# A two-layer encoder on one core: two Fourier sums and the token rows move to GpSimd, and the router, the first weight split and the final norm are reordered

## The reference, cut to what matters

```python
# layer 0
hn = rms_norm(h, norm_mix[0])
u = (hn @ w_in).reshape(B, S, 4, 256)
h = h + fft2(u, axes=(1, 3), norm="ortho").real.reshape(B, S, D) @ w_out
hn = rms_norm(h, norm_ffn[0]);  h = h + (silu(hn @ w_gate) * (hn @ w_up)) @ w_down
# layer 1
hn = rms_norm(h, norm_mix[1]);  h = h + neighbourhood_attention(hn, w_qkv, rpb, w_o)
hn = rms_norm(h, norm_ffn[1])
logits = hn @ w_router + b_router                 # 8 experts
top_val, top_idx = top_k(logits, 2);  gates = softmax(top_val)
h = h + sum over the two experts of gate * (silu(hn @ w_gate[e]) * (hn @ w_up[e])) @ w_down[e]
return rms_norm(h, final_norm)
```

## Time and profile before

| | us |
|---|---|
| median of 3 runs (1365.29 to 1366.33) | 1365.94 |
| the profiled execution, its own time | 1367.15 |
| its span from first to last instruction | 1365.3 |
| TensorE busy in the span | 1344.7 |
| VectorE, ScalarE, GpSimd busy | 1111.9, 923.2, 34.5 |

### The profile page before, as it was taken

The page is one execution under the profiler, slowest core; times in us unless marked ns, Lnnn a source line. Parts: engine busy times, 40 slices in busy tenths (PEclk is TensorE's granted clock), DMA queues, the critical chain, the costliest instruction groups (busy, mean ns, idle before and its releaser), DMA issues.

```text
span 1365.3 us, 17406 instructions
## 1 busy us (share of the span) xinstructions
PE 1344.7 (98%) x6341; PEld 1117.9 (82%) x6341; DVE 1111.9 (81%) x815; ACT 923.2 (68%) x755; POOL 34.5 (3%) x48
## 2 busy tenths in 40 slices
PE   8999999999999999999999999999999999999997
PEld 7888888787878888888888888888888888888885
DVE  5756666655678889888988988898898889889997
ACT  6554444545647778777777877877787787777774
POOL 0000000000101000000000000000000000002000
PEclk8999999999989999999999999999999999999999
DMA  9666775563339999999999999999999999999992
GB/s 354 246 207 179 210 211 190 175 204 104 101 109 378 383 378 365 395 382 357 398 388 372 373 394 377 358 398 388 368 376 394 367 370 397 381 374 385 396 394 90
DMA packets 194971, 432.32 MB, mean 317 GB/s; under 512 B 19632, under 2 KB 22064, under 8 KB 194800
## 3 DMA queue, kind: packets, MB, share of 16 engines
q1 hardware_dynamic: 178784, 416.28, 83.4%
q0 software_dynamic: 3360, 11.78, 2.2%
q10 hardware_dynamic: 12784, 3.69, 1.8%
HBM read 425.94 MB, written 5.78 MB: 316 GB/s over the span
## 4 chain that ended last, share of the span: by engine, by line
PE 95%; DVE 3%; ACT 1%; issue 1%; DMA 0%; POOL 0%; DVEq 0%; ACTq 0%
PE bank_G L1250 10%; PE bank_G L1252 10%; PE bank_G L1251 10%; PE bank_U L1250 10%; PE bank_U L1252 10%; PE bank_U L1251 10%; PE bank_Y L1250 8%; PE bank_Y L1252 8%; PE bank_Y L1251 8%; PE bank_T L1696 2%; PE bank_T L1250 1%; PE bank_T L1252 1%; PE bank_T L1251 1%; DVE w_lo L753 1%; PE bank_G L1512 0%
## 5 line engine op out<-in xcount | busy, mean ns | idle before, releaser
L753 DVE TENSOR_TENSOR w_lo<-raw,w_hi 128x2048 fp32r<-128x2048 f32 x390 | 885.9, 2289 | 184.6 <-ACT w_hi L458 183.8
L458 ACT ACTIVATE w_hi<-raw 128x2048 fp32r<-128x2048 f32 x390 | 748.6, 1920 | 276.6 <-PE bank_U L1252 98.2
L1250 PE MATMUL bank_Y<-w_hi,hidT_hi 128*128 128x512 f32 x492 | 192.2, 391 | 0.0
L1252 PE MATMUL bank_Y<-w_hi,hidT_lo 128*128 128x512 f32 x492 | 191.6, 389 | 0.0
L1251 PE MATMUL bank_Y<-w_lo,hidT_hi 128*128 128x512 f32 x492 | 191.5, 389 | 0.0
L1250 PE MATMUL bank_U<-w_hi,xg_hi 128*128 128x512 f32 x448 | 179.1, 400 | 0.0
L1250 PE MATMUL bank_G<-w_hi,xg_hi 128*128 128x512 f32 x448 | 175.2, 391 | 1.3 <-DVE xg_lo L774 0.9
L1252 PE MATMUL bank_U<-w_hi,xg_lo 128*128 128x512 f32 x448 | 175.0, 391 | 0.0
L1251 PE MATMUL bank_U<-w_lo,xg_hi 128*128 128x512 f32 x448 | 174.5, 390 | 0.0
L1252 PE MATMUL bank_G<-w_hi,xg_lo 128*128 128x512 f32 x448 | 174.5, 390 | 0.0
L1251 PE MATMUL bank_G<-w_lo,xg_hi 128*128 128x512 f32 x448 | 174.4, 389 | 0.0
(11 more groups left out here) (301 smaller groups left out, 1363.5 us busy)
## 6 DMA issues: line engine op xcount, KB each, us to landing
raw<-in_expert_w_gate SPq DMA_DIRECT2D x112, 1024.0 KB, 7.7
raw<-in_expert_w_up SPq DMA_DIRECT2D x112, 1024.0 KB, 7.8
raw<-in_expert_w_down SPq DMA_DIRECT2D x112, 1024.0 KB, 7.7
raw<-in_nat_w_qkv SPq DMA_DIRECT2D x12, 1024.0 KB, 5.1
raw<-in_ffn_w_gate SPq DMA_DIRECT2D x11, 1024.0 KB, 8.9
raw<-in_ffn_w_up SPq DMA_DIRECT2D x11, 1024.0 KB, 5.7
raw<-in_ffn_w_down SPq DMA_DIRECT2D x11, 1024.0 KB, 5.2
raw<-in_fourier_w_out SPq DMA_DIRECT2D x4, 1024.0 KB, 15.6
```

The costliest lines, as they stand in the source:

```text
L458: nc.scalar.activation(w_hi[w][:], raw[s][:], ACT.Copy).then_inc(hi_made, 1)
L753: nc.vector.tensor_tensor(w_lo[w][:], raw[s][:], w_hi[w][:].bitcast(f32), ALU.subtract).then_inc(lo_made, 1)
L1250: nc.tensor.matmul(out_, xh, wh, start=start, stop=False)
L1252: return nc.tensor.matmul(out_, xl, wh, start=False, stop=stop)
```

## The change

Seven edits. (1) 23 matmuls on zeros in place of 12. (2) VectorE's split of piece 5 moves from before the second `u_lo` to behind the rests of `token_dft` 0 to 3. (3) `token_dft` writes four banks in turn and `channel_dft` one of its own for each group; the sums over tokens are done by GpSimd. (4) The first product of a stream waits for each quarter by itself. (5) The router: the gain goes into the router's weights, the stream goes token block by token block between the `w_o` products (one of its four groups of transposes stands in the middle of `last_wo_product`), the logits of a block start when it is there, the splits of two later pieces come after the choice of slots, and more `keep_warm` matmuls run. (6) The normed rows `hn` are made by GpSimd, two instructions for each token block, before the first expert's gather. (7) In expert 7 the last weight piece is split by column halves and the first half of the result is scattered before the second is complete; the gain is multiplied in early by VectorE and the final scale is applied by ScalarE; three of six small weight instructions come later.

```diff
@@ start and Fourier part @@
-        still(12)
+        still(23)
@@ vector
-            split_past(at["w_in"][c][-1])
+            split_past(at["w_in"][c][-1] - c)
...
-            even, odd = Y[g % 2][:, :S], fo["odd"][:, g % 2]
+            even, odd = BY_CHANNEL[g][:, :S], fo["odd"][:, g % 2]
...
-            for n, op in enumerate((ALU.add, ALU.subtract)):
-                nc.vector.tensor_tensor(tokens[:, :, n], channels[:, :, 0], channels[:, :, 1], op).then_inc(ft_tokens, 1)
...
+            if g == 1:
+                split_past(at["w_in"][1][-1])
             if g >= 2:
+                dve.wait_ge(ft_tokens, 2 * (g - 1))
@@ gpsimd
+        rstds(0)
+        for g in range(GROUPS):
+            channels, tokens = fo["by_channel"][:, g % 2], fo["by_token"][:, g % 2]
+            pool.wait_ge(ft_channels, 2 * (g + 1))
...
+            for n, op in enumerate((ALU.add, ALU.subtract)):
+                nc.gpsimd.tensor_tensor(tokens[:, :, n], channels[:, :, 0], channels[:, :, 1], op).then_inc(ft_tokens, 1)
@@ tensor
-            if m >= 2:
-                pe.wait_ge(pt_lo_done, m - 1)
+            if m >= 4:
+                pe.wait_ge(pt_lo_done, m - 3)
@@ tensor, project()
+                        if stream is not None and b == 0 and kk % 2 == 0:
+                            pe.wait_ge(act_lo_done, 4 * stream + kk // 2 + 1)
@@ rows, gpsimd (before: line 1205 on vector)
+        for b in range(NB):
+            pool.wait_ge(rstd_done, 3 + b + 1)
+            pool.wait_ge(h_half, 4 + 2 * b + 2)
+            nc.gpsimd.tensor_scalar(hn[:, b], h[:, b], rstd[:, 3, b:b + 1], None, ALU.mult).then_inc(hn_scaled, 1)
+            pool.wait_ge(hn_scaled, b + 1)
+            nc.gpsimd.tensor_tensor(hn[:, b], hn[:, b], mo["gain"][:, 0], ALU.mult).then_inc(hn_made, 1)
@@ router, tensor
+        wo_product(0, 1, 0)
+        wo_product(1, 1, 0)
+        transpose_tokens_of(0, 0)
+        wo_product(0, 1, 1)
+        transpose_tokens_of(0, 1)
+        last_wo_product()
         pe.wait_ge(rw_lo_done, 1)
+        logits(0, 0)
+        transpose_tokens_of(1, 1)
+        logits(0, 1)
+        logits(1, 0)
+        logits(1, 1)
+        keep_warm(12)
...
-        keep_warm(2)
+        keep_warm(5)
@@ router, vector
+        nc.vector.tensor_tensor(mo["rw"][:], mo["rw"][:], gains[:, 3].unsqueeze(2).to_broadcast([P, KD, NE]), ALU.mult).then_inc(rw_scaled, 1)
...
+        add_wo(0, 0)
+        split_past(W0 + 2)
+        add_wo(0, 1)
+        squares_of_rest(0)
+        tokens_lo(0, 0)
+        token_lo(0, 0)
+        add_wo(1, 0)
+        tokens_lo(0, 1)
+        token_lo(0, 1)
+        tokens_lo(1, 0)
+        add_wo(1, 1)
+        squares_of_rest(1)
+        tokens_lo(1, 1)
@@ expert 7, tensor
+            if kept:
+                last_columns(0, 4)
+                last_columns(1, 2)
+                scatter(0)
+                last_columns(1, 2, 2)
...
+            if kept:
+                scatter(1)
@@ end, scalar
+        for q in range(2):
+            for b in range(NB):
+                act.wait_ge(e_added, NB * q + b + 1)
...
+                nc.scalar.activation(mo["hn_hi"][:, b, cs], h[:, b, cs], ACT.Square, accum_out=total).then_inc(fin_sq, 1)
+        for b in range(NB):
+            act.wait_ge(fin_rstd, b + 1)
+            for q in range(2):
...
+                nc.scalar.activation(part, part, ACT.Copy, scale=rstd[:, 4, b:b + 1]).then_inc(fin_scaled, 1)
@@ end, vector
-                nc.vector.scalar_tensor_tensor(out=hn[:, b, cs], in0=h[:, b, cs], scalar=rstd[:, 4, b:b + 1],
-                                               in1=mo["gain"][:, 1, cs], op0=ALU.mult, op1=ALU.mult).then_inc(fin_done, 1)
+            nc.vector.tensor_tensor(FINAL[b][:, cs], h[:, b, cs], mo["gain"][:, 1, cs], ALU.mult).then_inc(fin_gain, 1)
```

More of the change, by code:

```diff
@@ L1160, in expert @@
                     hidden_rest(E, c - 1)
+                if (kind, c, half) == ("gate", STEPS - 1, 1) and kept and not sweep:
+                    gate_weights()
                 if (kind, c, half) == ("gate", 1, 1) and ahead and not sweep:
@@ L1252, in three, with project @@
             return nc.tensor.matmul(out_, xl, wh, start=False, stop=stop)
-        def project(pieces, banks, width, done, before=lambda n, b: None):
+        def project(pieces, banks, width, done, before=lambda n, b: None, stream=None):
             for n, j in enumerate(pieces):
@@ L1720, in down, with last_columns, scatter @@
                 last.then_inc(piece_used, 1)
+            def last_columns(q, rows, first=0):
+                c = STEPS - 1
+                if first == 0:
+                    ready(AT["down", c, 0], E)
+                    pe.wait_ge(e_hidT_lo, E * STEPS + (c + 1))
+                for kk in range(first, first + rows):
+                    half, k = kk // KROW, kk % KROW
+                    j = AT["down", c, half]
+                    if q == 0 and half and k == 0:
+                        pe.wait_ge(lo_half, E - LAST + 1)
+                    if q == 1 and half and k == 0:
+                        ready(j, E)
+                    wh, wl = parts(j, E, KROW)
+                    cs = slice(BANK * q, BANK * (q + 1))
+                    last = three(Y[q][:], hidT_hi[c % 2][:, P * kk:P * (kk + 1)], hidT_lo[c % 2][:, P * kk:P * (kk + 1)],
+                                 wh[:, k, cs], wl[:, k, cs], False, kk == BANK // P - 1)
+                    if q and k == KROW - 1:
+                        last.then_inc(piece_used, 1)
+                    elif kk == BANK // P - 1:
+                        last.then_inc(e_y, 1)
+            def scatter(q):
+                pe.wait_ge(e_selT_copy, E - LAST + 1)
+                pe.wait_ge(e_ylo, 2 * (E - LAST) + 1 + q)
+                for b in range(NB):
+                    cs = slice(BANK * q, BANK * (q + 1))
+                    bk = T[q] if b == 0 else (G, U)[q][1]
+                    nc.tensor.matmul(bk[:], mo["selT"][:, b], mo["y_hi"][:, cs], start=True, stop=False)
+                    nc.tensor.matmul(bk[:], mo["selT"][:, b], mo["y_lo"][:, cs], start=False, stop=True).then_inc(e_scatter, 1)
             for c in range(STEPS):
```

303 lines of the change are left out of this document (167 added, 136 removed).

## The result

| | us |
|---|---|
| before, median of 8 runs | 1365.76 |
| after, median of 8 runs (1368.80 to 1372.45) | 1370.65 |
| ratio, 95% interval | 1.0032, 1.0023 to 1.0041 |
| profiled execution of after: own time, span | 1369.09, 1367.3 |

The change makes the kernel slower by 3.1 to 5.6 us. The forecast was 1360.0 with a range to 1366.8: wrong in sign, and outside the range.

What follows compares the result with a forecast made beforehand. TensorE, busy 1344.7 of 1365.3 us, was taken as the bound. Gains 2.25 - 1.2 + 0.85 + 3.7 + 0.4 + 0 = 6.0 were to bring the median from 1365.94 to 1360.0; own range 1357.5 to 1363, stated range 1357.8 to 1366.8.

Steps and rivals of the forecast that it cites:

- The normed rows: Router: GpSimd makes them in 6 us (bounds 3.8 to 7.5) beside VectorE's chain, which keeps its pace; cost 0.
- Rival 1: Router: GpSimd holds up VectorE's chain, nine instructions with two SBUF inputs; router loses 2.5, total 1366.2; chance 0.32.
- Rival 3: Router: GpSimd's rows take 9, VectorE is held until 398, router loses 5 or more; total 1369; chance 0.10.
- The router: Logits end earlier, `used` comes 3.0 earlier and the gather runs at full clock: gain 3.7.
- The start: More zero matmuls keep the clock at 2.4 GHz, so the Fourier part begins at 31.0, not 33.28: gain 2.25.
- The Fourier part: After the start: TensorE waits 1.05 for the last two groups and starts `w_out` 0.13 later: loss 1.2.
- GpSimd's 0.6 an instruction: Fourier part: assumed price of each GpSimd sum over tokens, between 0.38 (gain 0.3) and 0.94 (loss 3.9).
- the ring: Fourier part: each group passes `fold`, GpSimd's two sums, `act_hi`, `act_lo` and handovers, 3.35 us a round.
- The moved split: Fourier part: 2.3 us of VectorE work before the first `fold`, giving back part of what the start gives.
- Waits by quarters: At 257, first product of a stream: two `act_lo` suffice instead of four, removing most of a 1.36 wait: gain 0.85.
- Expert 7: Three of six weight instructions move away from TensorE's 0.4 wait for `w_lo`: gain 0.4, between 0 and 0.42.
- the end: After the last product: 0.95 lost to early scatter, 0.4 and 0.44 gained, 0 to 0.6 for GpSimd's root: taken as 0.

Runs made afterwards that it cites:

- E1: The changed kernel with the normed rows back on VectorE: median 1365.79, 0.9999 of before.
- E8: The kernel before with only the normed rows moved to GpSimd and VectorE's two instructions removed: median 1371.23, 1.0031 of before.
- E5: The changed kernel with both the normed rows and the Fourier sums by token back on VectorE: median 1363.45, 0.9977 of before.
- E2: The changed kernel with the Fourier sums by token back on VectorE: median 1369.24, 1.0020 of before.
- E3: The changed kernel with the final scalings back on VectorE behind the root, without early gain products: median 1370.32, 1.0027 of before.
- E4: The changed kernel run again unchanged, for a second profile: median 1371.17, 1.0030 of before.
- E6: As E5, with the weight split of piece 5 back in front of the second `u_lo`: median 1363.42, 0.9978 of before.
- E9: As E5, with the first half's scatter back behind the last down products: median 1364.25, 0.9986 of before.
- E10: As E5, with 12 zero matmuls at the start in place of 23: median 1365.67, 0.9996 of before.
- E15: The kernel before with 23 zero matmuls at the start in place of 12, nothing else: median 1366.02, 0.9997 of before.
- E16: E5's kernel run again unchanged: median 1363.58, 0.9976 of before.
- E13: As E5, with scatter behind the last down products, last scalings on VectorE and both `y_lo` ahead of the adds: median 1362.21, 0.9972 of before.
- E7: The changed kernel with GpSimd's normed rows held back until VectorE's last `hn_lo`: median 1367.58, 1.0008 of before.

## Why the prediction was wrong, point by point

- **The normed rows, "at 0", is the step that failed.** I wrote that "VectorE's chain runs at its own pace, at 0". It costs 4.2 to 5.4 us in the time (E1), 4.2 put into the kernel before by itself (E8). Two things were wrong in it. The direction: from one row in which GpSimd gave way to VectorE I took it that VectorE never does. It was the case in which VectorE had started first. The price: the four instructions take 10.4 us in place of 6, over my upper bound of 7.5 and my rival's 9, so that GpSimd is busy until 398.4, and its second product also meets `slot`, behind `used`; `sel` meets the clearing of `no_row` that follows.
- **The rivals.** Rival 1 had the mechanism, but counted only the nine instructions with two SBUF inputs; `slot` (and `sel`), `tensor_scalar` with one input, were held too. With 1366.2 it was short by 4.4. Rival 3 (0.10) had the price and the direction, 1369 against 1370.65, though not the sum: it had the router lose 5 and the rest gain 2.3. The Trainium skill's "SBUF — State Buffer", "Who interferes with whom", weighed in the forecast, was right where I set the row above it: of two engines on the shared pair the one that starts second waits, and `tensor_scalar` may take that pair as well. The trace agrees for GpSimd's product (`eq` and `slot` end with it) and for `tensor_reduce`, which was never held; GpSimd's scaling of 2.84 us, however, held VectorE only to its first 1.1.
- **The router, 3.7: right without the rows.** E1 gains 3.9 against the profile of before, E5 5.1. The chain took 3.0 for my 3.4. But the clock did not stay up: it fell within the logits or behind them in most profiles of the new router, for 3 to 7 us (some 10 in E2, and twice in E3 and E4), at another moment each time (E5, E6 and E9 kept it). And in the profiles with the rows on VectorE 1.4 to 1.7 are given back before the last result row, which I had not in the sum.
- **The start, 2.25: right for that execution, not for each.** 30.91 for 31.0 forecast. Against the profiles E8 and E10 it is 1.3, and by itself, with two banks, it gives no gain clear of noise (E15). With the rest of the change in place it is worth more than its stage shows, 2.6 by the ratios of E10 and E5; in E10's profile 1.3 of it stands at the start and the rest in a longer router, where the clock was low for 6.8 us (3.2 in E16); whether its other executions are like that, and why, these runs don't tell.
- **The Fourier part, loss 1.2: 2.8.** One mis-sized term is GpSimd's 0.6 an instruction: 0.72, eight of them, and the ring went round in 3.63 for 3.35, which makes about 1.0 of the 1.6. The rest is not GpSimd's price: with the sums on VectorE the loss is 0.6 (E2), where I had a gain of 0.3 for 0.38 an instruction. There TensorE waits 0.29 and 1.56 for `pt_lo` and starts the product with `w_out` 14.1 behind the first Fourier product, where the kernel before took 13.5. The moved split, which I blamed for "what the start gives", is worth nothing that can be measured either way (E6).
- **Waits by quarters, 0.85: 0.67.** Both first `act_lo` were enough, as forecast: the wait fell from 1.36 to 0.58.
- **Expert 7, 0.4, and the end, 0: together a loss of 1.2.** The 0.4 wait is gone, and up to the last product E13 is 0.7 shorter than the kernel before. For the end my own terms add up to a loss of 0.1 to 0.7, of which I took 0. By the profiles the early scatter put the last product off by 1.35 (E13 against the changed kernel) where I gave 0.95. From the end of the scatter to the last scaling it gained 0.3 where I had credited 0.84. And the last transfers landed 3.4 us behind the last scaling in place of 2.6, a term that I didn't have; E5 and E16, with the same end, have 2.7, so it isn't the end's edit alone. E13 shows that the order of before was the better one.
- **The sum.** Second profile of after against the profile of before: 2.3 - 2.8 + 0.7 - 2.8 - 0.1 - 1.2 = -3.9 by the rounded stages. The medians differ by 4.9, since the profiled execution of before stood 1.4 above its median and this one of after 0.4 above 1370.65. Between the 6.0 of the forecast and this -3.9 lie 9.9 us: 6.5 in the router, which is what taking the rows off GpSimd gives back there (6.6 in E1), 1.6 in the Fourier part and 1.6 in expert 7 and the end.

## What to carry to other kernels

Before work goes to GpSimd, write down which VectorE instructions run in the same microseconds, and count its single-input `tensor_scalar` among those that can be held; work that is free by its own dependences can sit on the critical path through what the two engines share. Here 2.5 us of VectorE work (the two `hn` instructions in E5), behind the last urgent split, was 4 to 5 us cheaper than 10.4 us on an "idle" engine. A short row that grows to the end of another engine's row shows it; the list of waits has only TensorE's longer wait for `sel`, not its cause. And take a gain from one profile's low clock with care: 3.4 and 6.8 us at half clock came from the same instructions.

The best kernel of the study is E13 (23 zero matmuls, four banks, waits by quarters, the new router, rows and sums on VectorE, the old end): 1362.21, 0.9972 of before, with an interval to 0.9984, and 0.6% under the changed kernel. E5, with only rows and sums back, has 0.9977.

## What the runs showed of the hardware

- GpSimd's `tensor_scalar` of 128 x 1024 with one scalar for each partition took 2.85, longer than its `tensor_tensor` of two such inputs, 2.36; 128 x 256 with two inputs took 0.72.
- VectorE's small instructions with two SBUF inputs, and its `tensor_scalar` with one, were held to the end of GpSimd's `tensor_tensor` (up to 2.27 of its 2.36; `tensor_reduce` was not), but only for the first 1.1 of its `tensor_scalar` (in the changed kernel, E4 and E8: VectorE's instruction starts within 0.1 of it and takes 1.06), and in the changed kernel VectorE then ran nine small instructions at full pace beside the rest of it. The other way, GpSimd's `tensor_scalar` was stretched from 2.86 to 7.00 beside VectorE's long rests (E7).
- The clock fell to 0.50 in the router of the changed kernel at 388 although TensorE had no idle in the windows before: its work there was the logits, products of 8 and 16 columns, and one group of transposes. E5, at 1.00 throughout, and E16, at 0.50 for some 3 us, are the same program; the router took 13.12 and 14.22.
